# Two transformer blocks on one core: every second low part of the merge's output product from an accumulating DMA

## What is computed

```
merged = sigmoid(g_a) * (y_a @ w_up_a) + sigmoid(g_b) * (y_b @ w_up_b)
x = x + merged @ w_o                 # <- the merge's output product, 256x2048 by 2048x2048
h = rmsnorm(x, ffn_norm_g)
hid = h @ w_ffn_in                   # the feed-forward part follows
```

## Time and profile before

| | |
|---|---|
| median of 3 runs | 2066.08 us (2065.88 to 2068.45) |
| profiled execution, span from first to last instruction | 2066.0 us |
| PE / DVE / ACT / POOL busy | 2053.2 / 1221.1 / 976.4 / 34.0 us |
| traffic of the DMA queue of SP | 376.10 MB, 55.3% of 16 engines |

### The profile page before, as it was taken

How to read it: one execution, slowest core, us unless ns; L and a number is a source line. 1 busy time by engine, 2 the same in 40 slices (tenths; PEclk the granted TensorE clock), 3 DMA queues, 4 the chain that set the end, 5 groups by cost and what they waited for, 6 DMA issues and landing times.

```text
span 2066.0 us, 24467 instructions
## 1 busy us (share of the span) xinstructions
PE 2053.2 (99%) x9445; PEld 1703.5 (82%) x9445; DVE 1221.1 (59%) x1304; ACT 976.4 (47%) x1221; POOL 34.0 (2%) x44
## 2 busy tenths in 40 slices
PE   8999999999999999999999999999999999999999
PEld 7888888888888888888888888888888888888887
DVE  5877776555666665655455554555555555555664
ACT  6545445544565456444444444344434443444453
POOL 1000000000001100000000000000000000000000
PEclk9999999999999999999999999999999999999999
DMA  8544354556556554455555555555555555555553
GB/s 278 169 139 162 128 199 143 190 184 210 190 183 204 183 164 162 163 183 189 197 183 196 181 175 197 188 184 189 195 183 185 191 192 183 190 192 187 183 184 122
DMA packets 191772, 377.09 MB, mean 183 GB/s; under 512 B 8482, under 2 KB 10196, under 8 KB 191572
## 3 DMA queue, kind: packets, MB, share of 16 engines
q1 hardware_dynamic: 191700, 376.10, 55.3%
HBM read 373.98 MB, written 2.10 MB: 182 GB/s over the span
## 4 chain that ended last, share of the span: by engine, by line
PE 97%; DVE 1%; ACT 1%; issue 0%; DMA 0%; SPq 0%; DVEq 0%; ACTq 0%
PE acc L854 61%; PE acc L859 31%; PE aux L837 2%; PE aux L918 1%; PE aux L828 1%; DVE wlo L1283 0%; DMA resid<-in_x 0%; PE aux L908 0%; PE aux L933 0%; DVE att_z L1783 0%; PE aux L1106 0%; PE aux L1116 0%; PE aux L1143 0%; DVE att_l L1781 0%; ACT whi L506 0%
## 5 line engine op out<-in xcount | busy, mean ns | idle before, releaser
L1283 DVE TENSOR_TENSOR wlo<-raw,whi 128x1024 fp32r<-128x1024 f32 x704 | 860.3, 1224 | 779.4 <-ACT whi L506 775.4
L506 ACT ACTIVATE whi<-raw 128x1024 fp32r<-128x1024 f32 x704 | 745.4, 1060 | 1051.0 <-PE acc L859 1039.7
L854 PE MATMUL acc<-whi,actA_hi 128*128 128x512 f32 x1472 | 581.2, 395 | 1.2 <-DVE actA_lo L1298 1.2
L854 PE MATMUL acc<-whi,actA_lo 128*128 128x512 f32 x1472 | 575.2, 391 | 0.0
L859 PE MATMUL acc<-wlo,actA_hi 128*128 128x512 f32 x1472 | 394.5, 390 | 0.0
L854 PEld LDWEIGHTS acc<-whi,actA_hi 128*128 128x128 f32 x1472 | 277.6, 189 | 58.2 <-DVE actA_lo L1298 1.6
L854 PE MATMUL acc<-whi,actB_hi 128*128 128x512 f32 x828 | 325.0, 393 | 0.0
L859 PEld LDWEIGHTS acc<-wlo,actA_hi 128*128 128x128 f32 x1472 | 277.1, 188 | 57.7
L854 PEld LDWEIGHTS acc<-whi,actA_lo 128*128 128x128 f32 x1472 | 277.9, 189 | 55.6
L854 PE MATMUL acc<-whi,actB_lo 128*128 128x512 f32 x828 | 322.5, 389 | 0.0
L859 PE MATMUL acc<-wlo,actB_hi 128*128 128x512 f32 x828 | 221.8, 390 | 0.7 <-DVE wlo L1283 0.6
(11 more groups left out here) (268 smaller groups left out, 1156.5 us busy)
## 6 DMA issues: line engine op xcount, KB each, us to landing
raw<-in_w_in SPq DMA_DIRECT2D x132, 1024.0 KB, 5.1
raw<-in_w_ffn_in SPq DMA_DIRECT2D x88, 1024.0 KB, 5.0
raw<-in_w_ffn_out SPq DMA_DIRECT2D x44, 1024.0 KB, 5.1
raw<-in_w_out SPq DMA_DIRECT2D x16, 1024.0 KB, 5.2
raw<-in_w_pg SPq DMA_DIRECT2D x16, 1024.0 KB, 5.2
raw<-in_w_o SPq DMA_DIRECT2D x16, 1024.0 KB, 5.1
raw<-in_w_ple_gate SPq DMA_DIRECT2D x16, 1024.0 KB, 5.2
raw<-in_w_up_a SPq DMA_DIRECT2D x8, 1024.0 KB, 5.1
```

Of the source, the lines that this page charges most:

```text
L506: act.activation(whi[:, g % RING], raw_piece(g), ACT.Copy).then_inc(hi_ready, 1)
L854: pe.matmul(acc2(n)[:, t, :], act[x][:, k + c, t * P:(t + 1) * P], whi[:, g % RING, c, :], start=(p == 0 and c == 0 and x == 0), stop=False)
L1283: dve.tensor_tensor(wlo[:, g % RING], raw_piece(g), whi[:, g % RING].bitcast(F32), ALU.subtract)\
```

## The change

In stage G the odd pieces of each slab (p = 1, 3, 5, 7; 16 of 32) no longer get their low part from DVE. ACT writes the high part as before and then, with scale -1 and in fp32r, the negated high part into wlo. POOL then issues a DMA that adds raw onto it (raw - hi), waits until it has landed, waits until all earlier low parts are counted, and counts up lo_ready in its place. These 16 steps stand in POOL's order ahead of the power for "ffn". DVE's subtraction of an even piece first waits until the DMA of the odd piece before it is counted; so does the first piece of F0. merge_second and add_slab keep their place behind p == 3 in DVE's loop, where the subtraction of piece 3 is gone. The same places of wlo, raw and whi are used.

```diff
@@ gpsimd, in the loop over POWS
+                if name == "ffn":
+
+                    for q in range(16):
+                        g = SLABS[FIRST["G"]][0] + 2 * q + 1
+                        pool.wait_ge(sem("neg_ready"), q + 1)
+                        pool.dma_start(wlo[:, g % RING].bitcast(F32), raw[:, g % RAW], accum_op=ALU.add)\
+                            .then_inc(sem("lo_added"), 16)
+                        pool.wait_ge(sem("lo_added"), 16 * (q + 1))
+                        pool.wait_ge(lo_ready, g)
+                        pool.sem_inc(lo_ready, 1)
@@ scalar
+            def split_neg(g):
+
+                split_hi(g)
+                act.activation(wlo[:, g % RING], raw_piece(g), ACT.Copy, scale=-1.0).then_inc(sem("neg_ready"), 1)
...
-                    split_hi(SLABS[FIRST["G"] + s][0] + p)
+                    split_neg(SLABS[FIRST["G"] + s][0] + p) if p % 2 else split_hi(SLABS[FIRST["G"] + s][0] + p)
@@ vector
                 dve.wait_ge(hi_ready, g + 1 + i * ROUND)
+                if SLABS[FIRST["G"]][0] < g <= SLABS[FIRST["F0"]][0] and g % 2 == 0:
+                    dve.wait_ge(lo_ready, g)
...
-                    split_lo(SLABS[n][0] + p)
+                    if p % 2 == 0:
+                        split_lo(SLABS[n][0] + p)
```

## The result

The changed kernel takes 2115.25 us (median of 4 runs, 2113.15 to 2117.36), against 2066.93 us for the kernel before; the ratio is 1.0233, 95% interval 1.022 to 1.0247. It is 48 us slower. The forecast was 2068 us, no change to be measured, with 2094 as the upper end of the range. The profiled execution's span is 2112.2 us, 46.2 above that of before; its own time is 2113.87, so 1.7 us lie around the span. (The prediction took under 0.1 for that.)

What follows compares the result with a forecast made beforehand. PE was taken to bound the kernel (busy 2053.2 of 2066.0 us). Negation's end to lo_ready, 5.1 + 0.3 + 0.6 = 6.0 us, loses 2.0 us: 2066.1 + 2 = 2068 us, range 2065 to 2094.

Steps and rivals of the forecast that it cites:

- PE is never kept waiting before, so nothing can be gained: Stage G: PE busy 94.00 of 94.00 us, idle 0.0 us before low matmuls, so a removed subtraction frees no PE time.
- (a): DVE in stage G: removing 16 subtractions of 1225 ns, 19.6 us, is worth nothing to the end.
- (b): ACT in stage G: 16 added negating copies, 17 us, are covered by 51.4 us of idle time and cost nothing.
- (d): Odd pieces' lo_ready moved to POOL, with DVE and loads waiting: loads still land 9 us early; nothing, unless transfers crowd.
- The thresholds and the formula for the loss: Stage G, x from negation's end to lo_ready: largest of three stalls, none to 4.9 us; at low matmuls 16x - 95.3.
- x: the DMA by itself: POOL's DMA, negation's end to lo_ready: accumulate counted as 1 MB of traffic, 5.1 us, plus 0.3 for POOL's steps.
- rival 1: Stage G: the DMA flies between two load bursts, 3.3 to 4.9 us to lo_ready, wholly hidden; 2066.1 us; chance 0.2.
- x: sharing with the loads: DMA engines in stage G: half a load burst met at half speed adds 0.6 us to the DMA, at most 2.3.
- Rival 2: Stage G: POOL's serial DMA chain is longer than PE's 5.82 us beat; 2075 to 2107 us; chance 0.42.
- Rival 3: Stage G: only the first DMA is late, over 9.0 us, stalling PE at the merge; 2070 to 2073 us; chance 0.06.
- Rival 4: Stage G: crowded transfers make ACT wait for raw; a small addition to the slow-chain case, no chance of its own.
- The check-list: Profile after, stage G: 16 more ACT copies, 16 fewer subtractions, 8 MB new queue, landing 5 to 6 us, PE waits.

Runs made afterwards that it cites:

- Experiments 7: Changed kernel, but only pieces 3 and 7 of each slab (8 of 32) use negation and DMA, DVE subtracts the other 24: 2066.87 us, ratio 0.9998.
- experiment 8: Changed kernel without negation and DMA: POOL itself subtracts the high part from raw for the odd pieces, same waits and counts: 2066.80 us, ratio 0.9998.
- experiment 9: Changed kernel without POOL's DMAs: ACT negates as before, DVE adds raw onto it and counts lo_ready: 2067.39 us, ratio 1.0001.
- experiments 1: Changed kernel with weight loads issued on stage G's counts cut to 32 of 512 columns, all accumulating DMAs kept: 2068.17 us, ratio 1.0004.
- experiment 2: Changed kernel with the 16 DMAs as plain copies of raw onto wlo instead of accumulates: 2087.66 us, ratio 1.0107.
- experiment 4: Changed kernel with the loads of stage G waiting for one low part more, same bytes and accumulates: 2074.48 us, ratio 1.0033.
- experiment 5: Changed kernel with plain copies instead of accumulates and stage G's loads one low part later: 2068.44 us, ratio 1.0004.
- experiment 6: Changed kernel, but POOL issues the next odd piece's DMA before waiting for and counting the one before, so two may be in flight: 2079.09 us, ratio 1.0057.

## Why the prediction was wrong, point by point

- **PE is never kept waiting before, so nothing can be gained**: right. Experiments 7 to 9 free DVE of 8 or 16 subtractions, or leave it all of them, and all three are level with before.
- **(a) and (b), subtractions worth nothing, negations hidden**: right (experiment 9).
- **(d), the moved counts cost nothing by themselves**: right (experiment 8). But the part on the loads is where it went wrong. I asked only whether a later load would still be in time, and it is: ACT never waits for raw. I did not ask what the load does to the DMA that is issued on the same count.
- **The thresholds and the formula for the loss**: right. 16x - 95.3 gives 45.5 of 46.2 us with the measured x, and with values of x that were estimated beforehand it placed experiments 1, 2 and 4 within 2 us. It does not give the 6 us of the profiled execution of experiment 5.
- **x: the DMA by itself**: right. I counted an accumulate as 1 MB of traffic, 5.1 us, with 0.3 for POOL, together 5.4; the first one took 5.2 to its count and alone they land in 4.5, 0.6 under the 5.1. The Trainium skill's two rules (DMA: Bandwidth & Descriptors, on the DMA of the gpsimd path; Collectives: The Full Stack, on an add's two reads) gave estimates of 3.2 for a copy and 4.4 for an accumulate; alone they measured 2.9 and 4.5. The rules agree with the traces within 0.3 us for a DMA that has the engines to itself; as rival 1 they failed, since here it does not.
- **x: sharing with the loads, the step that failed.** The sum had 0.6 us for it ("half of the burst met at half speed") and 2.3 as its bound. Measured: 8.4 - 4.5 = 3.9 us, and 6.8 - 2.9 = 3.9 for the copy. Two things were wrong in it. The bound rested on fair sharing of a 2.3 us burst; in fact the DMA got its turn behind nearly the whole load, and a load is 3.2 us of engine time (0.55 x 94 over 16 loads; the 2.3 counted only the stretch in which the engines were full) and some 4 in the lock. And the meeting was not chance: the text itself noted that "the next DMA meets the next burst", because one count releases both, yet priced it as a half meeting. Once POOL is behind, each DMA is issued 0.5 us after a load, every time.
- **Rival 2, POOL's chain longer than PE's beat (0.42)**, is what happened, past its last priced value: x = 8.8 instead of up to 8.5, and 2115 instead of 2107. It named full engines as its cause. Experiments 2 and 5 show that fullness was not needed: in experiment 2 the engines are a third idle (share 0.67 from 1150 to 1220 us) and 20 us are lost all the same, and in experiment 5 the same bytes in the other order lose nothing. Fullness is at most a smaller, second limit, within the 7 us of experiment 4.
- **Rival 3, a slow first DMA**: wrong. It took 1.07 us on POOL instead of 0.87 and landed in 4.8 us, the fastest of the 16. **Rival 4, starving loads**: wrong.
- **The check-list**: 16 copies more, 16 subtractions fewer, 8 MB on a new queue and PE waiting at the low matmuls of odd pieces were as described; "landing 5 to 6 us" and "PE idle before the transposes of merged" were not.

## What to carry to other kernels

Two transfers that are released by the same semaphore count don't overlap by chance; in this kernel they met every time, and the one that was issued second got the other's whole length on top. So price a DMA on a deadline as its own landing time plus the whole of the transfer that its own completion releases (here 4.5 + 3.2 and 2.9 + 3.2, each still 0.7 us short of the 8.4 and 6.8 measured), and when that exceeds the beat, move the one with slack behind the one without: here one low part later for the loads gave back 41 of 48 us. Add up engine time per beat as well: where an accumulate (twice a copy) and the load came to more than the beat, 7 us stayed lost in the better order, and with copies none. A subtraction that nobody waits for is no reason to move anything; if it must leave DVE, POOL did it in 2.4 us for nothing.

## What the runs showed of the hardware that was not expected

- A DMA issued 0.5 us behind a 1 MB load loses 3.9 us, whether it is an accumulate or a copy, against the load's 3.2 us of engine time; the load ahead loses only 1.4 (5.1 to 6.5). With the order reversed the accumulate loses 1.2 (4.5 to 5.7) and the load 2.4 (5.1 to 7.5). Between these two runs the larger loss is on whoever comes second: by queue, the 16 engines serve one transfer almost to its end before they turn to the other.
- An accumulating DMA of 512 KB within on-chip memory keeps all 16 engines for 2.9 us, a copy for 1.3. POOL is occupied 0.87 us by issuing the one and 0.54 by the other.
- The lock is entered, not built in: with accumulates the third DMA is the first to wait for the count of the one before, with copies the fourth.
- In the stalled stage the granted clock fell to a mean of 0.90, with waits of up to 4 us at PE. It cost nothing that the sum misses, as PE was not the one setting the pace; with waits of about 2 us at most it stayed at 1.00 in experiment 6 (1150 to 1220 us) and had a mean of 0.98 in experiment 4.
